# Two transformer blocks on one core: gain row, recurrence copies and the down projection's raw weight tiles

## The reference

```python
# first block
h = rms_norm(x, pre_norm_w)
p = h @ w_in                          # 8320 columns: recurrence, convolution, pooling, gates
y_a = rwkv7_branch(...)               # 8 heads of 64, a recurrence over 1024 tokens
y_b, y_c = short_conv_branch(...), pool_branch(...)
merged = sum over n of sigmoid(gate_n) * (y_n @ w_branch[n])
x = x + rms_norm(merged @ w_out, post_norm_w)
# second block
proj = rms_norm(x, attn_norm_w) @ w_in_2   # windowed attention and two-way retention
h = x + concat(y_attn, y_ret) @ w_out_2
m = rms_norm(h, ffn_norm_w)
out = h + (silu(m @ w_gate) * (m @ w_up)) @ w_down      # hidden width 2816
```

## Time and profile before

| | us |
|---|---|
| median of 3 runs | 2244.04 (2243.98 to 2244.3) |
| the profiled execution, whole time | 2244.64 |
| its span, first to last instruction | 2242.9 |
| PE busy | 2218.5 (99%) |
| DVE busy | 1554.3 (69%) |
| ACT busy | 837.8 (37%) |
| POOL busy | 476.1 (21%) |

### The profile page before, as it was taken

The page is one execution under the profiler, slowest core; times in us unless marked ns, Lnnn a source line. Parts: engine busy times, 40 slices in busy tenths (PEclk is TensorE's granted clock), DMA queues, the critical chain, the costliest instruction groups (busy, mean ns, idle before and its releaser), DMA issues.

```text
span 2242.9 us, 30930 instructions
## 1 busy us (share of the span) xinstructions
PE 2218.5 (99%) x11960; PEld 1835.1 (82%) x11960; DVE 1554.3 (69%) x2646; ACT 837.8 (37%) x1486; POOL 476.1 (21%) x379
## 2 busy tenths in 40 slices
PE   9999999999999999999999999999999999999998
PEld 7778788777788888888888888888888888887777
DVE  6775886778858444665448777754776666678998
ACT  5334243333444334223334454542333333345441
POOL 2000000000002321143122212200122222236552
PEclk9999999999999999999999999999999999999999
DMA  4122221221233334853221212133222222233334
GB/s 151 44 57 53 64 58 35 62 56 58 65 113 116 113 113 150 291 169 129 91 72 52 59 38 59 39 127 113 76 85 85 85 78 82 85 115 106 107 122 149
DMA packets 254547, 208.55 MB, mean 93 GB/s; under 512 B 49985, under 2 KB 223681, under 8 KB 254402
## 3 DMA queue, kind: packets, MB, share of 16 engines
q1 hardware_dynamic: 254400, 206.58, 29.6%
q10 hardware_dynamic: 2, 0.00, 0.0%
HBM read 151.48 MB, written 47.71 MB: 89 GB/s over the span
## 4 chain that ended last, share of the span: by engine, by line
PE 79%; DVE 14%; issue 2%; DMA 2%; SPq 1%; POOL 1%; ACT 1%; DVEq 0%; POOLq 0%; ACTq 0%
PE PS L120 77%; PE PS L123 3%; DVE Nn L129 2%; DVE Ntmp L129 2%; SPq L146 1%; DVE Wlo L129 1%; DMA Nn<-scr_ns 1%; DVE acc L129 1%; DMA wSrcA<-in_w_down_dram 1%; DVE wSrcS L129 1%; DVE Zt L129 1%; DVE cy L137 1%; DVE ST L137 1%; POOL wLoA L129 0%; DVE Xs L129 0%
## 5 line engine op out<-in xcount | busy, mean ns | idle before, releaser
L120 PE MATMUL PS<-Hhi,Wlo 128*128 128x512 f32 (+1 forms) x1304 | 421.4, 390 | 0.0
L120 PE MATMUL PS<-Hlo,Whi 128*128 128x512 f32 (+1 forms) x1304 | 420.5, 389 | 0.0
L120 PE MATMUL PS<-Hhi,Whi 128*128 128x512 f32 (+1 forms) x1304 | 419.5, 388 | 0.9 <-DVE Hlo L129 0.9
L120 PEld LDWEIGHTS PS<-Hhi,Whi 128*128 128x128 f32 x1304 | 240.3, 189 | 45.9 <-issue 2.0
L120 PEld LDWEIGHTS PS<-Hhi,Wlo 128*128 128x128 f32 x1304 | 239.1, 189 | 45.9 <-issue 2.4
L120 PEld LDWEIGHTS PS<-Hlo,Whi 128*128 128x128 f32 x1304 | 239.6, 189 | 44.9 <-issue 2.2
L126 ACT ACTIVATE Whi<-Wraw 128x512 fp32r<-128x512 f32 x170 | 106.4, 629 | 333.7 <-PE PS L120 333.3
L129 DVE TENSOR_TENSOR Wlo<-Wraw,Whi 128x512 fp32r<-128x512 f32 x166 | 121.4, 734 | 73.2 <-ACT Whi L126 72.4
L129 DVE TENSOR_TENSOR Ntmp<-Nn 32x30 f32<-32x30 f32 (+14 forms) x240 | 76.7, 319 | 23.3 <-DMA Nn<-scr_ns 17.1
L129 POOL TENSOR_TENSOR sm<-sm,expo 128x8 f32<-128x8 f32 x8 | 17.3, 2165 | 340.4 <-DVE sm L134 340.3
L129 DVE TENSOR_TENSOR Nn<-Nn,Ntmp 32x30 f32<-32x30 f32 (+14 forms) x240 | 76.6, 319 | 6.9
(11 more groups left out here) (497 smaller groups left out, 5216.8 us busy)
## 6 DMA issues: line engine op xcount, KB each, us to landing
Wraw<-in_w_in_dram SPq DMA_DIRECT2D x126, 256.0 KB, 2.9
scr_g<-stg SPq DMA_DIRECT2D x24, 512.0 KB, 3.1
tg<-scr_g SPq DMA_DIRECT2D x24, 512.0 KB, 4.3
scr_fb<-fb SPq DMA_DIRECT2D x22, 512.0 KB, 4.1
gwA<-in_w_in_dram SPq DMA_DIRECT2D x40, 256.0 KB, 3.4
wA<-in_w_gate_dram SPq DMA_DIRECT2D x38, 256.0 KB, 3.2
wA<-in_w_up_dram SPq DMA_DIRECT2D x38, 256.0 KB, 3.3
wSrcA<-in_w_down_dram SPq DMA_DIRECT2D x48, 192.0 KB, 2.9
```

The costliest lines, as they stand in the source:

```text
L120: return self.h.matmul(out, lhsT, rhs, start=start, stop=stop, skip_group_check=True)
```

## The change

It does four things. (1) Entry: POOL sets all of `xn[1]` to zero before the gain row lands in its first partition, and `xn[2]` holds zeros with a row of 32 in place of the row of ones, so the gain matmul has 128 rows. 5 warm-up matmuls stand before it and 2 behind. ACT squares the first token tiles before it copies the gain, and the norms of tiles 0 and 1 read the gain from PSUM. (2) Recurrence: the copies of the upper half of `av` and the transposing copy `Nt` move from DVE to ACT. (3) Down projection: A11, A21, A22, A12 have a second set of raw tiles, taken by odd blocks, and SP waits for the block before last; the first odd block's tiles wait for the last plain product ("fu", 21). (4) All streams are woven in new orders, with new bank picks.

```diff
-WARM = (4, 8)
+WARM = (5, 2)
...
+def last_in_source(b):
+
+    i = b[1] - (2 if b[0] == "w" else 1)
+    return (b[0], i) if i >= OPEN[b[0]][1] else None
...
+        W.wsrc_odd = {name: mw(f"wSrc{name}1", [128, 3, 128]) for name in ("A11", "A12")}
+        mw = Bump(nc, R1 + 61440, R2)
+        W.wsrc_odd |= {name: mw(f"wSrc{name}1", [128, 3, 128]) for name in ("A21", "A22")}
...
+    def source(self, name, b):
+
+        P = self.bp[b[0]]
+        return P.wsrc_odd[name] if b[0] == "w" and b[1] % 2 and name[0] == "A" else P.wsrc[name]
...
+        pe.wait_ge(*S.start_dve.at("one"))
         pe.wait_ge(*S.grow_dma.at(0))
         for j in range(2):
-            bank, _ = banks.take(("gain", j), (f"SB{j}",), [S.init_act.at("gain")])
-            t = pe.mm(bank, K.xn[0][0:1, 0:128], K.xn[1][0:1, j * 512:j * 512 + 512])
-        t.then_inc(*S.xtr_pe.tick("gain"))
+            bank, _ = banks.take(("gain", j), (f"SB{j}",), [S.init_act.at("gain"), S.xn_dve.at((1, j))])
+            pe.mm(bank, K.xn[2][:, 0:128], K.xn[1][:, j * 512:j * 512 + 512]).then_inc(*S.xtr_pe.tick(("gain", j)))
...
-                bk, before = banks.take(("av", u, g), SIDE, [S.stage_act.at(("a", u, g)), S.stage_dve.at(("v", u, g))])
+                bk, before = banks.take(("av", u, g), SIDE, [S.stage_act.at(("a", u, g))])
...
     def begin():
+        act.wait_ge(*S.xrstd_pool.at("row"))
         act.dma(K.xn[1][0:1, :], K.D["pre_norm_w"]).then_inc(*S.grow_dma.tick(0, by=16))
         yield
-        act.wait_ge(*S.xtr_pe.at("gain"))
+        act.wait_ge(*S.xtr_pe.at(("gain", 1)))
+        act.wait_ge(*S.xn_dve.at((1, 1)))
...
-                act.act(K.WU[0:64, :, 4 * g:4 * g + 4, 0:64], src[0:64], ACT.Copy).then_inc(*S.stage_act.tick(("a", u, g)))
+                act.act(K.WU[0:64, :, 4 * g:4 * g + 4, 0:64], src[0:64], ACT.Copy).then_inc(*S.stage_act.tick())
+                act.act(K.WU[64:128, :, 4 * g:4 * g + 4, 64:128], src[64:128], ACT.Copy).then_inc(*S.stage_act.tick(("a", u, g)))
...
+            act.wait_ge(*S.inv_dve.at(("dg", u)))
+            if u:
+                act.wait_ge(*S.xtw_dma.at(u - 1))
+            act.act(K.Nt, K.Nn[0:16].rearrange("p s t -> p t s"), ACT.Copy).then_inc(*S.stage_act.tick(("nt", u)))
+            yield
...
+                gain = banks.of(("gain", keys[0][1])) if i < 2 else K.g_row[:]
+                if i < 2:
+                    dve.wait_ge(*S.xtr_pe.at(("gain", keys[0][1])))
...
-                dve.cp(K.WU[64:128, :, 4 * g:4 * g + 4, 64:128], src[64:128]).then_inc(*S.stage_dve.tick(("v", u, g)))
...
     def token_norms():
+        pool.memset(K.xn[1][:], 0.0).then_inc(*S.xrstd_pool.tick("row"))
+        yield
...
         for b in BLOCKS:
             kind, P = b[0], K.bp[b[0]]
             start = b == OPEN[kind]
+            last = last_in_source(b)
...
+            elif last is None:
+                sp.wait_ge(*S.dense_pe.at(("tile", ("fu", 21))))
             else:
-                sp.wait_ge(*S.sum_dve.at(("S3", (kind, b[1] - 1))))
-                sp.wait_ge(*S.sum_dve.at(("S4", (kind, b[1] - 1))))
-                sp.wait_ge(*K.sum_lo("A11", (kind, b[1] - 1)))
+                sp.wait_ge(*S.sum_dve.at(("S3", last)))
+                sp.wait_ge(*S.sum_dve.at(("S4", last)))
+                sp.wait_ge(*K.sum_lo("A11", last))
...
-                if sig is S.s1_dma and not start:
-                    sp.wait_ge(*K.sum_lo("A22", (kind, b[1] - 1)))
+                if sig is S.s1_dma and last is not None:
+                    sp.wait_ge(*K.sum_lo("A22", last))
+                if kind == "w" and not start:
+                    sp.wait_ge(*sig.at((kind, b[1] - 1)))
...
 ORDER = {
     "pe":
-        "a5d24a2d14a2d36a2d7a2d27a2d10a2d78pd5pd8pd18id3pd20id7s2d5s2d4pd5pd9pd19id41pd5id7s2d4sd7s2d5s2d5scs"
+        "a4d18a3d17a2d22a2d8a2d20a2d10ad2ad99pd4pd8pd20id3pd19sdsd3s2d5id4pd4pd8pd16id61pd4id9s2d4sd5s2d3s2d3"
...
     "act":
-        "Z2q2aw2aqaqwa2wa3q2a3qaqa5wew2ewep5wpwepw2ews4wfp5wpwfpw4fws3wfs4ws6wpfwgwep4wgps2wesps2ws2wesws4wsp"
+        "Zq2wqawaZawa2wqa2qa2qa3qa5wew2ewep5wpwepw2es2ws2p2wfp3wp2wfw4fwswfs3ws7wsfs2pw2egp4wgpswepws2wesws8"
...
     "sp":
-        "x2w2xwxwx2wx2lw10i2wiw6i2wi3fiwi2w4i2wi2wigw3i2wiw3gfw3i2wi3wi3w3fwiwi2wi2gw3i2wiw6i2wi2wifigiwiw2fw"
+        "x2wxwxwxwx2wxlw11i3w7fi2wi3wi3w5gi2wi2wiwi2wiw3fw3i4wi2gi2w4fwgi2wi3w6i3wgw5fwi2wi6w2fw3gi2wi2wiwi2w"
...
-        "GS2GS2G2wF4S2F4GS2F4GF4S4F2SFSF5S2FSF2SFS2FSF2SF5S2FSF2SFS2FSF2SFu8S2u2Su2SuSu2Su10",
+        "2F4GF4S2F4GS7FSF2SF5S3F3SFS3F3SF5S2FSF2SFS2FSF2SFu8S3u17",
```

More of the change, by code:

```diff
@@ L1255, in begin @@
     def begin():
+        act.wait_ge(*S.xrstd_pool.at("row"))
         act.dma(K.xn[1][0:1, :], K.D["pre_norm_w"]).then_inc(*S.grow_dma.tick(0, by=16))
         yield
-        act.wait_ge(*S.xtr_pe.at("gain"))
+        act.wait_ge(*S.xtr_pe.at(("gain", 1)))
+        act.wait_ge(*S.xn_dve.at((1, 1)))
         for j in range(2):
-            act.act(K.g_row[:, j * 512:j * 512 + 512], banks.of(("gain", j)), ACT.Copy, scale=32.0).then_inc(*S.init_act.tick("gain"))
+            act.act(K.g_row[:, j * 512:j * 512 + 512], banks.of(("gain", j)), ACT.Copy).then_inc(*S.init_act.tick("gain"))
         yield
@@ L1789, in block_weights @@
                     act.wait_ge(*S.dense_pe.at(("half", N_BACK[kind] - NSPL + (c - 3))))
-                act.act(P.slots[name][0][:, 0:width(b), :], P.wsrc[name][:, 0:width(b), :], ACT.Copy).then_inc(*S.sum_act.tick((name, b)))
+                act.act(P.slots[name][0][:, 0:width(b), :], K.source(name, b)[:, 0:width(b), :], ACT.Copy).then_inc(*S.sum_act.tick((name, b)))
                 yield
@@ L1825, in begin @@
     def begin():
-        dve.memset(K.xn[0][0:1, 0:128], 1.0).then_inc(*S.start_dve.tick("one"))
         dve.memset(K.xse[:, :, 1024:1025], float(np.sqrt(1024 * EPS))).then_inc(*S.start_dve.tick("eps"))
         dve.memset(K.Whi[NSPL - 1][:].bitcast(F32), 0.0).then_inc(*S.start_dve.tick("zero"))
+        dve.memset(K.xn[2][:, 0:128], 0.0).then_inc(*S.start_dve.tick("rows"))
+        dve.wait_ge(*S.start_dve.at("rows"))
+        dve.memset(K.xn[2][0:1, 0:128], 32.0).then_inc(*S.start_dve.tick("one"))
         dve.memset(K.expo[:], -0.5).then_inc(*S.start_dve.tick("expo"))
@@ L1841, in token_norms @@
     def token_norms():
-        dve.wait_ge(*S.init_act.at("gain"))
         for i in range(8):
+            if i == 2:
+                dve.wait_ge(*S.init_act.at("gain"))
             if i >= NXN:
@@ L2059, in invert @@
             yield
-            if u:
-                dve.wait_ge(*S.xtw_dma.at(u - 1))
-            dve.wait_ge(*S.inv_dve.last())
-            dve.cp(K.Nt, Nn[0:16].rearrange("p s t -> p t s")).then_inc(*S.inv_dve.tick(("nt", u)))
-            yield
     def stage():
@@ L2074, in stage @@
             yield
-            for g in range(2):
-                src = banks.of(("av", u, g)).rearrange("p (c h f) -> p h c f", c=4, h=2)
-                dve.wait_ge(*S.stage_pe.at(("av", u, g)))
-                if u:
-                    dve.wait_ge(*S.stage_pe.at(("de", u - 1, 1, 1)))
-                dve.cp(K.WU[64:128, :, 4 * g:4 * g + 4, 64:128], src[64:128]).then_inc(*S.stage_dve.tick(("v", u, g)))
-                yield
             for g in range(2):
@@ L2602, in block_weights @@
                     at = (slice(None), slice(0, width(b)))
-                    dve.tt(P.slots[name][1][at], P.wsrc[name][at], P.slots[name][0][at].bitcast(F32), ALU.subtract).then_inc(
+                    dve.tt(P.slots[name][1][at], K.source(name, b)[at], P.slots[name][0][at].bitcast(F32), ALU.subtract).then_inc(
                         *sums.tick(("lo", name, b)))
@@ L2617, in block_weights @@
                 at = (slice(None), slice(0, width(b)))
-                dve.tt(P.wsrc[step][at], P.wsrc[x][at], P.wsrc[y][at], op).then_inc(*sums.tick((step, b)))
+                dve.tt(K.source(step, b)[at], K.source(x, b)[at], K.source(y, b)[at], op).then_inc(*sums.tick((step, b)))
                 yield
@@ L3058, in block_weights @@
                         part = src[k0:k0 + 512, :].rearrange("(k p) n -> p k n", p=128)
-                    sp.dma(P.wsrc[name][:, 0:width(b), :], part).then_inc(*sig.tick(b, by=16))
+                    sp.dma(K.source(name, b)[:, 0:width(b), :], part).then_inc(*sig.tick(b, by=16))
                 yield
@@ L3219 @@
+        "iw3fwgw3i4wifi3w3fw2gfwi3wi2fw2fw2fwS2Gw2GwgcGSGSFGSGS2G2S2G2S2G2S2G2S2G2S2G2S2G2SG2b4F2w3GwGF3wbFbF"
+        "2wFbFwbFwFbwFbwFwFwbwFbwFwFwFbwFwFwFwFwmwmwmwmwm4w3nr2srsrsrsrsrsrs2w3kw3kwow4ow2kw2ow4ow2kw2ow3ow2k"
+        "w3ow4ow5t3wtw2t3wtnr2s2r2s2r2srsrs2S2w2Sw2G2S3GS2GS2GS2GS2GS2GS2GS2GS2GS2GS2GS2GS2GS2GS2GS2GS2G2wF4S"
+        "2F4GF4S2F4GS7FSF2SF5S3F3SFS3F3SF5S2FSF2SFS2FSF2SFu8S3u17",
 }
 PICKS = (
[L3221 removed]
```

110 lines of the change are left out of this document (54 added, 56 removed).

## The result

The changed kernel takes 2252.51 us in the median of six runs (2251.45 to 2254.29), the kernel before 2244.17 (2243.5 to 2246.02). The ratio is 1.004, with a 95% interval of 1.003 to 1.005. The forecast was 2235.0, in a range of 2230 to 2240.5. Its sign was wrong.

The account below looks back on a forecast made before the run. PE, busy 2218.5 of 2242.9 us, bounds the kernel, so only its standing and half clock can go. Down projection 5.8 + entry 1.8 + recurrence 1.5 = 9.1 us gives 2235.0 us, range 2230 to 2240.5.

Parts of the forecast that it names:

- Entry: Start of the kernel: first product of real data at 13.1 against 14.91 us, gain 1.8 us, bounds 0.2 to 2.8.
- The warning on the clock: At the entry: if PE's clock isn't up at 13.1 us, up to 1.7 us are lost, nearly cancelling the gain.
- Recurrence: 40 to 700 us: gain 1.5 us, 0.8 for half clock and 0.7 for DVE's stalls; bounds 6 gain, 6 loss.
- rival (c): Recurrence: new order with emptier DVE removes most stalls, 6 instead of 1.5 us, 2230.4 in all; chance 0.13.
- Rival (b): Recurrence: ACT's queue, serial copies of `av` banks plus half-clock stretches make it slower, 2251 at full price; chance 0.08.
- Down projection: 2011.3 to 2235.6 us: second raw-tile set removes weight-sum waits and half clock, gain 5.8 us, bounds 1 to 6.9.
- The chain from raw tile to S4: Down projection, block 3: raw tiles land, DVE makes sums up to S4, ACT rounds; too late by some 2 us.
- Rival (a): Down projection: DVE's full queue or block 1's late tiles limit the gain to 1 to 3 us, 2240.0; chance 0.13.
- First odd block: Down projection, block 1: later tiles, S4 ready at 2022.5, wanted at 2023.5; cost nothing, bounds 0 to 2 us.
- Attention stage: Attention stage: the new orders have the same steps, so nothing gained or lost.
- Tail: Behind the last product: 7.4 us of adding, transposing and storing, a chain of its own, so nothing.
- the three signs of being wrong: PE's waits move to hB11 or wHiA; PE idle passes 12 us in 40 to 700; more than two half-clock stretches.

Follow-up runs that it names:

- after: The whole change, all four parts, against the kernel before: 2252.51 us, ratio 1.004.
- the front kernel: Changed kernel with the old orders and bank picks from the recurrence's end on and one set of raw tiles: 2236.74 us, ratio 0.9971 to the kernel before.
- the twelve runs on its base: Twelve follow-up kernels, all with the changed kernel's front, its copies and orders, varying later orders or raw-tile sets: medians 2234.54 to 2245.07 us.
- the one with three places moved back: Front kernel plus new attention orders, PE's side steps later at four places, the first not past the score product: 2240.26 us, ratio 0.9986 to the kernel before.
- The early order alone: Front kernel, one raw-tile set, block 3's weight sums moved up: 2241.24 us; with S4's low part also moved in blocks 3 and 4: 2239.94 us.

## Why the prediction was wrong, point by point

**Entry, -1.8 forecast, -1.50 measured. Right,** and nearly by its own working: the gain's matmuls started at 5.45 us (5.0 taken), took 3.75 (3.78), the first multiplication came at 7.63 (6.9), the first product at 13.40 (13.1). Over all runs of this code it lay between 12.55 and 13.76. The warning on the clock was right too: after lost part of 13.7 to 17 us to 1.2 GHz, while the front kernel ran there at full clock with the same instructions.

```profile
5.45 3.75 PE L120 MATMUL PS<-xn,xn 128*128 128x512 f32 x4 [1.48 <-DMA xn<-in_pre_norm_w_dram]
...
7.63 0.75 DVE L137 SCALAR_TENSOR_TENSOR xn<-xs,ss,PS 128x512 f32<-128x512 f32 x1 [5.81 <-PE PS L120]
...
13.40 0.36 PE L120 MATMUL PS<-Hhi,Whi 128*128 128x256 f32 x1 [0.69 <-DVE Hlo L129]
```

**Recurrence, -1.5 forecast, -3.8 measured in after, and between -3.8 and -6.5 in the twelve runs on its base. Undersized.** The sign and the source were right: PE's idle time fell by 3.4 us, inside the 5 to 9 that the forecast allowed, the waits for Xs from 2.5 to 0.6 us and for rk from 2.2 to 1.0, and the half clock at 325 us went. I had given each an even chance or less; both came. The -3.8 of after still hold 1.7 us of loss: its stretch at 1.2 GHz from 13.7 us on lies behind the first product. The mechanism is rival (c)'s, whose terms give 2244.0 - 1.8 - 6 = 2236.2 for the front kernel, which took 2236.74. Whether the emptier DVE or the new orders did it is not shown. Rival (b), a full queue on ACT, did not show, though ACT got 32.4 us more work and not 18.3. WU has its 80 copies, as forecast, but the transposing copy of Nn takes ACT twice DVE's 1107 ns, where I had taken DVE's price for lack of an ACT row:

```profile
L126 ACT ACTIVATE Nn<-Nn 16x1024 f32<-16x1024 f32 x8 | 16.9, 2108 | 11.8 <-DVE Nn L133 11.7
```

No wait of PE in this stage is seen to come from it; ACT is busy for 41% of the time.

**Down projection, -5.8 forecast, +6.1 measured. The step that failed is the sum's silence on what the new order puts behind the weight sums.** The chain from raw tile to S4 came out as costed. The tiles of block 3 were issued in pairs at 2026.9 and 2029.9 us (before 2030 was the mark set), and S4 was made 2.8 us before the block began, where before it was made 4.9 us into it. The waits for wHiS and wLoS fell to 1.0 us, under the 1.5 of the forecast, and block 3 lost its 3.8 us. But the page had 91% of DVE busy in this stage, and I used that only to trim the gain by 1.1 us. On a queue so full every step moved up moves others back. The steps that gave way were the sums of the hidden tiles, which feed a ring over four engines: PE waited 6.0 us for hB11lo and ran two stretches at half clock. The forecast named "PE's waits move to hB11" as a sign of failure, but gave it no place in the sum and no rival. Rival (a) came nearest; it had 1 to 3 us of gain at its worst, no loss.

**First odd block, 0 forecast (0 to 2), 1.3 measured in after. In the bounds.** The microsecond to spare wasn't there: block 1 took 10.81 us instead of 9.52. Under the old orders it would have been 2.9 us, in block 0; with block 1 left in the first set it is nothing.

**Attention stage, costed at nothing, +7.5 measured. The step that failed is "the same steps, so nothing".** I read that the steps of this stage are the same and didn't read where they stand. In the kernel before, PE stands less than 1.2 us there in all. In the new order side steps ask too soon and wait, and with so little idle time nothing in the stage can give that back. The run with the old orders of this stage alone (466.02 us) and the one with three places moved back (468.85) show both the price and the cause of more than half of it. The cause of the rest is open.

**Tail, 0 forecast, +0.4 measured.** It comes with the new orders of the down projection: 8.11 to 8.13 us in the three kernels that have them, 7.65 to 7.68 in all others. It was not followed further.

**Sum.** -1.50 - 3.82 + 7.47 + 6.07 + 0.44 - 0.08 = 8.58 us of span. Slower got 0.08 of the chance, all of it on ACT's queue. That rival's price, 2251, is 1.5 us from the measured 2252.5 by luck, since its mechanism did not show. Two of the three signs of being wrong came: waits for hB11, and three stretches at half clock. Orders that are replaced as a whole, in stages where PE is 98 to 99% busy, ought to have carried a rival of their own, at the price of a few stalls of 2 us with half clock behind each.

## What to carry to other kernels

Where each engine runs a hand-made order, a change of that order is a change of the kernel, even where no instruction changes; here two such changes cost 7 to 8 us each, one in a stage whose work the change did not touch at all. (Bank picks changed with both. In the attention stage 4.1 us came back with the picks as they were, in block 4 3.7 us; what the picks cost is not shown.) Price a second buffer together with the order that uses it. Here the buffer alone brought nothing that the intervals show, and cost 2.9 us where its first load was put ahead of others. The early order alone cost 3 to 4.5 us, and both together were no better than the buffer alone (2234.54 and 2235.05 us). On a queue that is 90% busy, name for each step that moves up the step that it passes, and follow that one to the engine that needs it.

The best kernels of this study keep the front of the change, the old orders behind it, and a second set that only the even blocks from 2 on use: 2235.05 us, and 2234.54 with blocks 3 and 4 rearranged, against 2242.7 to 2244.5 for the kernel before beside them. With one set it is 2236.74. These three are not told apart by their intervals.

## What the runs showed of the hardware that I had not expected

**POOL and DVE don't share, they take turns, and both show it.** In the timeline of block 4 above, POOL's hB21lo (2064.03, 1.80 us) is on while DVE's T1 starts at 2064.63; T1 takes 1.75 us, where the form alone takes 0.68, and ends 0.55 us after POOL has ended. Then DVE's next sum starts at 2066.49 and takes its plain 0.69, and it is POOL's hB11lo, started 0.04 us after it, that takes 1.78. Whoever comes second pays most of what the other has left: T1 took 1.07 us longer with 1.20 of POOL's to go, and POOL's hB11lo some 0.5 longer than its 1.30 elsewhere, with 0.65 of DVE's to go. The Trainium skill says just this (SBUF — State Buffer, "Terms", on the shared port pair: the loser "fully blocks"), and the trace agrees, with 1.75 for 0.68 us. In the sum of the prediction it was a reason for doubt, by the 1.53 us of one weight sum; in the ring of block 4 it lengthens T1 and the low part behind it, the two steps that PE waits for last.

**The clock after a stall.** A stall of about 2 us of PE was followed by a stretch at 1.2 GHz in one execution and not in another. With the same stall in block 3 (1.9 us and 1.8 us for wHiS) the front kernel has, from 2040 to 2050 us,

```profile
2040.00:2050.00 10.00, 8.08 (x29) 6.07 (x28) 5.57 (x8) 4.30 (x9) 6.29 (x6) 0.83 0.49 149
```

and the one with two sets, block 1 in the first, and the old orders

```profile
2040.00:2050.00 10.00, 8.17 (x36) 6.34 (x35) 7.05 (x9) 5.02 (x11) 7.12 (x6) 1.00 0.53 159
```

The kernel with four places of PE's order moved in the attention stage has the front kernel's down projection, and with a stall of 1.9 us its block 3 takes 16.55 us, against 18.16 in the front kernel. Each such stretch is worth 1.7 us, as in the earlier trace rows. In this kernel that is the size of most of the effects under study, so a difference of under 2 us between two profiled executions says little before their clocks have been compared.
